# One decoder layer with routed experts, on one core: output projection and routing in one block, weight buffers shared, picks in batches of six tiles, block table through TensorE

## The reference

```python
mix = concatenate([y_conv, y_rec]) @ w_out
x = layer_norm(ALPHA * x + gate1 * mix, ln_g[0], ln_b[0])      # x1
u = x * (1.0 + scale2) + shift2                                # u2
# routing: top group of 4, top 2 of its 8 experts, 32 experts
p_group = softmax(xt @ w_rg); grp = argmax(p_group)
le = the 8 logits (xt @ w_re) of that group
top_p, top_i = top_k(softmax(le), 2)
wts = p_sel * top_p / sum(top_p)
# each expert: blocks of up to 128 tokens
h = silu(xblk @ w_gate[ex]) * (xblk @ w_up[ex]); y = h @ w_down[ex]
x = layer_norm(ALPHA * x + gate2 * y_moe, ln_g[1], ln_b[1])
```

## Time and profile before

| | us |
|---|---|
| median of 3 runs (1959.23 to 1959.64) | 1959.36 |
| the profiled execution, its own time | 1958.05 |
| its span | 1956.5 |

### The profile page before, as it was taken

How to read it: one execution, slowest core, us unless ns; L and a number is a source line. 1 busy time by engine, 2 the same in 40 slices (tenths; PEclk the granted TensorE clock), 3 DMA queues, 4 the chain that set the end, 5 groups by cost and what they waited for, 6 DMA issues and landing times. The chain is left out here.

```text
span 1956.5 us, 29481 instructions
## 1 busy us (share of the span) xinstructions
PE 1760.3 (90%) x9152; PEld 1374.9 (70%) x9153; DVE 1143.1 (58%) x1864; ACT 616.6 (32%) x770; POOL 597.1 (31%) x685
## 2 busy tenths in 40 slices
PE   5999999999999999999689989139999999999674
PEld 3888878888888899999478777127666777666331
DVE  4566665556666766565467778714456333455198
ACT  3333332222333222222211110205465434455142
POOL 0122222111222222102145556413444333344155
PEclk8999999999999999999799989569999999999897
DMA  8444334443333232331664342558899864798495
GB/s 262 140 141 131 115 99 139 131 133 111 98 99 91 87 87 59 90 108 41 218 187 151 130 130 98 166 176 275 282 358 339 310 231 167 252 315 301 194 387 182
DMA packets 302076, 342.76 MB, mean 175 GB/s; under 512 B 19077, under 2 KB 257446, under 8 KB 299537
## 3 DMA queue, kind: packets, MB, share of 16 engines
q1 hardware_dynamic: 278872, 284.30, 45.3%
q0 software_dynamic: 18000, 55.87, 7.9%
q10 hardware_dynamic: 5106, 1.31, 0.4%
HBM read 276.86 MB, written 64.58 MB: 175 GB/s over the span
## 5 line engine op out<-in xcount | busy, mean ns | idle before, releaser
L1534 DVE TENSOR_TENSOR w_gu_lo<-w_gu_raw,w_gu_hi (+1 forms) x64 | 146.4, 2291 | 158.3 <-ACT w_gu_hi L1527 158.2
L896 DVE TENSOR_TENSOR w_lo<-w_raw,w_hi 128x1024 fp32r<-128x1024 f32 x112 | 138.1, 1236 | 139.4 <-ACT w_hi L546 136.7
L658 POOL TENSOR_TENSOR o_r<-o_ms,neg_half 128x4 f32<-128x4 f32 (+1 forms) x16 | 16.8, 1051 | 663.0 <-DVEq L932 663.0
L1907 PE MATMUL ph<-w_gu_hi,x_hi 128*128 (+1 forms) x408 | 178.6, 438 | 12.9 <-DVE hh L1869 10.4
L713 PE MATMUL pr<-ub_hi,w_hi 128*128 128x288 f32 (+1 forms) x672 | 189.2, 335 | 0.0
L713 PE MATMUL pr<-ub_hi,w_lo 128*128 128x288 f32 (+1 forms) x672 | 184.2, 328 | 0.0
L713 PE MATMUL pr<-ub_lo,w_hi 128*128 128x288 f32 (+1 forms) x672 | 183.6, 327 | 0.0
L713 PE MATMUL pr<-ua_hi,w_hi 128*128 128x512 f32 x448 | 182.6, 408 | 0.0
L1935 PE MATMUL py<-w_dn_w,hhT 128*128 x400 | 180.9, 595 | 0.8 <-ACT hhT L1839 0.4
L713 PE MATMUL pr<-ua_hi,w_lo 128*128 128x512 f32 x448 | 177.0, 395 | 0.0
L713 PE MATMUL pr<-ua_lo,w_hi 128*128 128x512 f32 x448 | 176.9, 395 | 0.0
(11 more groups left out here) (334 smaller groups left out, 3482.5 us busy)
## 6 DMA issues: line engine op xcount, KB each, us to landing
w_raw<-in_w_in SPq DMA_DIRECT2D x112, 512.0 KB, 4.2
w_gu_raw<-in_w_e_gate SPq DMA_DIRECT2D x32, 1024.0 KB, 8.3
w_gu_raw<-in_w_e_up SPq DMA_DIRECT2D x32, 1024.0 KB, 11.9
w_dn_w<-in_w_e_down SPq DMA_DIRECT2D x32, 1024.0 KB, 10.1
w_mod<-in_w_mod SPq DMA_DIRECT2D x16, 1024.0 KB
y_t<-y_scratch SPq DMA_DIRECT2D x16, 1024.0 KB, 7.1
w_ring<-in_w_mod SPq DMA_DIRECT2D x4, 2048.0 KB, 17.4
x_cols<-in_x_prompt SPq DMA_DIRECT2D x32, 256.0 KB, 5.5
```

The source lines that it names most:

```text
L658: pool.tensor_tensor(o_r[:, 0:c], o_ms[:, 0:c], keep["neg_half"][:, 0:c], ALU.pow).then_inc(o_rs, 1)
L896: dve.tensor_tensor(w_lo[:, n % WS], w_raw[:, n % WRAW], w_hi[:, n % WS].bitcast(F32), ALU.subtract).then_inc(lo_done, 1)
L1534: dve.tensor_tensor(w_slot(keep["gu_lo"], s, lo, hi), w_slot(keep["gu_raw"], r, lo, hi), w_slot(keep["gu_hi"], s, lo, hi).bitcast(F32), AL ...
L1907: last = pe.matmul(ph[:, :], x[:, half, k * P:(k + 1) * P], w_slot(w, s, k * GU, (k + 1) * GU), start=(k == 0 and m == 0), stop=(k == KT - ...
```

## The change

- Output and routing become one block. The batches are (0,6), (6,12), (12,15) and (15,17); the first two are picked within the tile loop, the other two after it.
- In the tile loop, DVE's order per tile was residual, norm, `lo(t+3)`, picks; now it is residual, `lo(t+3)`, picks, norm. ACT makes `hi(t+2)` ahead of `to_sb(t-2)`, not behind it.
- u2 of tile 16 is made by DVE (`modulate_last`), not POOL.
- w_out, z, x1 and the transposes of u2 lie in the buffers of the gate and up weights (`gu_raw`, `gu_hi`, `gu_lo`). Gate and up weights of expert 0 are loaded at t = 8, those of 1 and 2 after the last logits; all three down weights are loaded in the expert phase.
- The table is transposed by two PE matmuls and copied by DVE from PSUM; it no longer goes to DRAM.
- Gate, norm weights and x1 of the first 8 tiles of the combine phase are loaded in the expert phase.

```diff
-    BATCH = ((0, 4), (4, 8), (8, 12), (12, 15))
+    BATCH = ((0, 6), (6, 12), (12, 15), (15, TILES))
...
-        wo_raw = sb("wo_raw", [P, KT, D])
+        wo_raw, wo_hi, wo_lo = (keep[n][:, 0:2, :].rearrange("p s (k d) -> p (s k) d", d=D) for n in ("gu_raw", "gu_hi", "gu_lo"))
+        mod_s = wo_raw[0:NSAMP, 4:7, :]
+        late = keep["gu_raw"][:, 2, :].rearrange("p (k d) -> p k d", d=D)
+        z, z2, x1 = late[:, 0, :], late[:, 1, :], late[:, 2:4, :]
...
                     if t + 2 < T:
                         load_x(t + 2)
+                    if t == 8:
+                        sp.wait_ge(list_out, 16)
+                        load_gate_up(sp, io, keep, 0, 0)
                     store(t)
...
+                sp.wait_ge(lg_ps, T)
+                for e in range(1, RAW):
+                    for landed in ("wg_in", "wu_in"):
+                        sp.wait_ge(keep[landed], 16 * e)
+                    load_gate_up(sp, io, keep, e, e)
...
                 for t in range(2, T):
-                    to_sb(t - 2)
                     if t + 2 < T:
                         hi(t + 2)
+                    to_sb(t - 2)
                     keep_logits(t - 2)
...
-                                scatter_rows(pool, R, scr, a + 2 * h, a + 2 * h + 2, sc_out)
+                                scatter_rows(pool, R, scr, a + 3 * h, a + 3 * h + 3, sc_out)
...
+                pe.wait_ge(tab_rdy, 1)
+                for c in range(2):
+                    last = pe.matmul(rk[0:1, c * P:(c + 1) * P], tab_f[:, c:c + 1], ident[:, :], start=True, stop=True)
+                last.then_inc(tab_ps, 1)
...
                 for t in range(T):
                     residual(t)
-                    norm(t)
                     if t + 3 < T:
                         lo(t + 3)
-                    dve.drain()
...
+                    norm(t)
+                    dve.drain()
...
+                modulate_last()
+                a, b = BATCH[2]
+                dve.wait_ge(lg_sb, b)
+                pick_groups(dve, R, a, b, gd_rdy)
+                pick_first(dve, R, a, b)
+                pick_second(dve, R, a, b, dm_rdy, mm_rdy)
+                place_rows(dve, R, rk, a, b, gs_rdy, w_rdy, rk_rdy, 2, dest_rdy)
...
-                sp.wait_ge(tab_rdy, 1)
-                sp.dma_start(scr["tab"], tab_i[:, :]).then_inc(tab_out, 16)
-                sp.wait_ge(tab_out, 16)
-                sp.dma_start(blk_tab[:, :], scr["tab"].rearrange("(a g) c -> a (g c)", a=1)).then_inc(tab_in, 16)
...
+                dve.wait_ge(tab_ps, 1)
+                dve.tensor_copy(blk_tab[:, :], rk[0:1, 0:2 * P])
                 dve.drain()
                 for e in range(2):
                     for a in range(2):
                         split_low(dve, keep, e, a, e, e)
...
+                for e in range(RAW):
+                    if e:
+                        sp.wait_ge(wd_in, 16 * e)
+                    load_down(sp, io, keep, e, e)
                 sp.wait_ge(xg_in, 32)
...
+                for t in range(EARLY):
+                    tail(NE - 2 + t // 4, t % 4, P, scr["x1"][t * P:(t + 1) * P, :])
```

More of the change, by code:

```diff
@@ L1310, in _ @@
                             pair_shares(act, R, a, b, w_rdy)
-                for t in range(T - 2, T):
-                    to_sb(t)
-                    keep_logits(t)
+                to_sb(LAST - 1)
+                keep_logits(LAST - 1)
+                act.wait_ge(gd_rdy, 3)
+                group_shares(act, R, *BATCH[2], gs_rdy)
+                to_sb(LAST)
+                keep_logits(LAST)
+                act.wait_ge(dm_rdy, 3)
+                pair_shares(act, R, *BATCH[2], w_rdy)
+                act.wait_ge(gd_rdy, 4)
+                group_shares(act, R, *BATCH[3], gs_rdy)
+                act.wait_ge(dm_rdy, 4)
+                pair_shares(act, R, *BATCH[3], w_rdy)
+                for e in range(2):
+                    act.wait_ge(keep["wg_in"], 16 * e + 16)
+                    act.wait_ge(keep["wu_in"], 16 * e + 16)
+                    for a in range(2):
+                        split_high(act, keep, e, a, e, e)
             @block.gpsimd
@@ L1365, in _ @@
                         pool.wait_ge(list_out, 16)
-                    for i, (a, b) in enumerate(BATCH[0:3]):
+                    for i, (a, b) in enumerate(BATCH[0:2]):
                         for h in range(2):
@@ L1424, in _ @@
                     route(t - 2)
-                    for i, (a, b) in enumerate(BATCH):
+                    for i, (a, b) in enumerate(BATCH[0:2]):
                         if t == b + 3:
@@ L1513, in load_gate_up @@
[L1513 to L1527, removed]
@@ L1758, in down, with tail @@
                     load_down(sp, io, keep, e, s)
+                def tail(e, i, n, rows):
+                    sp.wait_ge(gu_l, 2 * e + 2)
+                    sp.dma_start(gu_raw[0:n, e % RAW, i * D:(i + 1) * D], rows).then_inc(tail_in, 16)
+                for e in range(RAW):
+                    if e:
+                        sp.wait_ge(wd_in, 16 * e)
+                    load_down(sp, io, keep, e, e)
                 sp.wait_ge(xg_in, 32)
@@ L1765, in _ @@
                 down(NE - 1, (NE - 1) % RAW)
+                for i, row in enumerate((scr["mod"][0, 3 * D:4 * D], None, io["ln_g"][0, 1], io["ln_b"][0, 1])):
+                    if row is not None:
+                        tail(NE - 3, i, P, row_bcast(row, P))
+                for b in range(DEC_B):
+                    sp.dma_start(gu_raw[b * DEC_L:(b + 1) * DEC_L, (NE - 3) % RAW, D:2 * D],
+                                 row_bcast(scr["mod"][b + 1, 3 * D:4 * D], DEC_L)).then_inc(tail_in, 16)
+                for t in range(EARLY):
+                    tail(NE - 2 + t // 4, t % 4, P, scr["x1"][t * P:(t + 1) * P, :])
+                sp.wait_ge(tail_in, 16 * (3 + DEC_B + EARLY))
             @block.gpsimd
@@ L1886, in expert_of @@
                 def expert_of(b):
-                    return pe.value_load(blk_tab[0:1, bass.ds(2 * b, 1)], min_val=0, max_val=NE - 1)
+                    return pe.value_load(blk_tab[0:1, bass.ds(b, 1)], min_val=0, max_val=NE - 1)
                 def transposes(b, half):
@@ L1967, in combine_phase @@
         ps_n = ps("ps_n4", [P, D])
-        in_ = [sem("t4_in%d" % s) for s in range(R)]
+        y_in = [sem("y4_in%d" % s) for s in range(R)]
+        x_in = [sem("x4_in%d" % s) for s in range(R)]
         o_out = [sem("o_out%d" % s) for s in range(4)]
@@ L1975, in rows_of, with x1_of @@
             return NSAMP if t == LAST else P
+        def x1_of(t):
+            n = rows_of(t)
+            if t < EARLY:
+                return tail[0:n, t // 4, (t % 4) * D:(t % 4 + 1) * D]
+            return x1[0:n, (t - EARLY) % R, :]
         with nc.Block() as block:
```

221 lines of the change are left out of this document (92 added, 129 removed).

## The result

The changed kernel takes **1984.3 us** (median of 4 runs, 1980.4 to 1985.8), the one before 1959.5 (1959.2 to 1959.7). The ratio is 1.0124, with a 95% interval of 1.0106 to 1.0141: the change makes the kernel 24.8 us slower. The profiled execution has a span of 1982.7 us against 1956.5, 26.2 more.

The account below looks back on a forecast made before the run. PE was taken to bound the output phase before, and the ring after the change. Terms 43.4 - 14.8 + 4 - 1.3 = +31.3 on 1958.05 gave 1989.4, with 1.3 to the median 1991 us; range 1966 to 2012.

Parts of the forecast that it names:

- X(16): End of x1 of tile 16, the last in the output phase: forecast at 1273.5 us against 1230.1 before, +43.4.
- The ring: Tile loop: x1, u2, its store, next y load, hi, lo, norm, x1 set the pace, 16.2 us per tile; chance 0.68.
- X(0): End of x1 of tile 0, at the output phase's start: forecast at 995.5 us against 991.2 before.
- The picks: DVE's routing picks, now between lo and norm in the tile loop: 18.6 us added at t = 7, 8, 9 and 13.
- Scatters: Six on POOL behind u2 at t = 11 and 12 delay the root by 1.4 us each, 2.8 in all.
- The hole: Stretch between output phase and experts, X(16) to the first list fetch: 45.3 us instead of 60.1, -14.8.
- The first blocks: Start of the expert phase: down weight loads beside the list fetch and gather that PE awaits, +4 us, ends 0 and 10.
- Combine: Combine phase: fewer bytes to load ahead of PE at tile 0, -1.3 us, and no gain behind it, where DVE bounds.
- the clock: Rival: PE idles in every tile of the output phase and its clock falls; 17.3 us per tile, 2005 us, chance 0.20.
- The faster ring: The same as rival 3: in the tile loop the ring turns faster than PE; 1929 us, chance 0.08.
- the cancelling: Rival: the tile loop's loss is small and cancels the hole's gain, within 4 us of before; chance 0.04.
- rival 3: Output phase: u2 and load under 8.5 us together, PE stays the bound, picks hidden; 29 us less, 1929; chance 0.08.

Follow-up runs that it names:

- e9: The changed kernel with the picks of the tile loop behind norm(t), lo(t+3) still ahead of norm: 1969.7 us, ratio 1.0047.
- e5: e1 with DVE's four splits of the first two experts' weights moved behind the barrier, into the expert phase: 1928.4 us, ratio 0.9858.
- e1: The changed kernel with SP asking for each y piece one tile earlier, ahead of the stores: 1935.2 us, ratio 0.9877.
- e3: The kernel before with only DVE's lo(t+3) moved ahead of norm(t): 1989.7 us, ratio 1.0156.
- e7: The changed kernel without the eight x1 tiles loaded ahead of the combine phase: 1985.0 us, ratio 1.0137.
- e2: The changed kernel with only DVE's lo(t+3) moved back behind norm(t): 1936.7 us, ratio 0.9888.
- e10: The changed kernel with SP issuing the load of x(t+2) ahead of that of y(t+3): 2008.1 us, ratio 1.0239.

## Why the prediction was right

The forecast was 1991 us, the measured time 1984.3; the sum was +31.3 us on the profiled execution, and it shows +26.2. Term by term, from the two timelines:

| term | forecast | measured |
|---|---|---|
| X(16) | +43.4 | +45.0 |
| X(16) to the first list fetch | -14.8 | -15.4 |
| first fetch to first transposes | +4 | +0.8 |
| first transposes to combine | 0 | -1.8 |
| combine to first zw | -1.3 | -2.2 |
| first zw to the end | 0 | -0.2 |

- **The ring.** Forecast 16.2 us per tile; the turn shown takes 16.1. The terms as listed add up to 16.3 and not to 16.2, which is 1.2 us over twelve tiles and changes nothing else. The parts measured: u2 store 5.85 us behind X (forecast 6.1), SP 0.4, the y load 5.0 to the start of `hi` (median of the 13 loads of the loop, 4.1 to 8.0; the view of landings has only five of them, 4.1 to 6.6, median 4.8), and the same `hi`, `lo` and norm. The queueing that I assumed beside u2 is in the rows: POOL's first step runs to 1052.56, DVE's step with two SBUF operands, which asks at 1051.49, ends at 1053.64, so that its 1.23 us fit in only from 1052.4 on, within 0.15 us of POOL's end; POOL's addition, issued at 1052.71, ends at 1055.90, 2.3 behind that. By the Trainium skill, "SBUF — State Buffer", section "SBUF: two separate sides", the two engines hold their shared port pair in turns, each for a whole instruction; these rows agree, with 2.15 and 3.19 us where 1.23 and 2.34 stand alone.
- **The y load.** The Trainium skill's fit ("DMA: Bandwidth & Descriptors", section "Anatomy of one DMA — SWDGE (gpsimd) path"), which the prediction weighed, would by an estimate have made the load 3.2 us and the total some 20 us lower. Both traces have about 5 us, on SP's queue and beside other transfers: the row was the right one to go by.
- **Slow y loads.** One was forecast, beside the filling of the list: 8.6 instead of 4.8 us. It is there in the turn to tile 2, 8.0 us from issue to `hi`, and that turn took 19.1 us, 3.0 above 16.1 (forecast 3.8). Three more weren't: in the turns to tiles 5, 10 and 12 it took 6.2, 6.6 and 6.2 us, and the turns were 17.2, 17.6 and 17.3. What slowed these isn't shown.
- **X(0)** came 4.8 us behind the forecast of 995.5. Of these 3.2 were there before the phase began: SP issued its first y load at 954.68 against 951.46, behind phases whose instructions the diff leaves alone; why they took longer isn't shown. From X(0) to X(13) it took 231.3 us, forecast 234.0. So the two parts of X(16) are off by +4.8 and -2.7, and the agreement at X(16) is better than its parts.
- **The picks.** The turns with picks at t = 7, 8 and 9 took 21.0, 19.2 and 21.3 us: 4.9, 3.1 and 5.2 above 16.1 (forecast 5.1, 3.1, 5.3); the one at t = 13, with the half piece of y, 19.2 (forecast 19.5). e9 shows what their place costs.
- **Scatters** at t = 11 and 12: the turns took 16.4 and 17.3, forecast 17.6 each, and the step forecast for them is mostly wrong. The root behind six scatters held x1 of tile 11 for 0.53 us; at tile 12 it ended at 1209.06, while DVE was still in `lo`, and held nothing. The 1.2 us of that turn lie in the y load. So 0.5 us came the way forecast, of 2.8.
- **Tiles 14 to 16** took 43.5 us, forecast 44.0, with x1 of the last tile held 8.0 us for the root behind six scatters.
- **The hole.** 44.7, forecast 45.3. The table's way through PE, which the trace of before didn't show and which was taken as 1.6, took 1.5 from the matmuls to the end of the copy. The splits became the last link, as forecast; e5 takes them out.
- **The first blocks** are the term that was mis-sized: +4 forecast, +0.8 measured. I charged to the first list fetch what such a fetch takes more in the expert phase's traffic, 3.8 us. The down loads start at 1317.70, 2.1 us ahead of the first fetch, but POOL had to wait for it only 3.54 us against 2.69 before. In e1 this stretch took 10.1 us, in e3, without the down loads there, 9.1.
- **Expert phase.** -1.8 us is no effect that I can claim: with the same matmuls this stretch took 539.4 to 545.2 us over the twelve kernels. What makes it vary stays open.
- **Combine.** -1.3 forecast; -2.2 between the two profiled executions, and -1.4 between the means of the nine kernels with the changed phase and the three with the old one. The size is near, the mechanism isn't shown: the forecast gave it to x1 being there early, and e7, without those loads, keeps all but 0.3 us. That the term came out is luck.

Of the rivals, the clock (0.20) fell as what sets the time, but the granted clock did go down as PE waited more. The windows from about X(0) to X(13), the changed kernel and then e1:

```profile
1000.00:1231.00 231.00, 197.20 (x928) 161.18 (x929) 131.34 (x176) 28.45 (x45) 90.26 (x52) 0.91 0.40 132
1000.00:1180.00 180.00, 178.01 (x924) 150.33 (x925) 126.36 (x176) 27.69 (x44) 95.26 (x52) 0.99 0.51 166
```

Nearly the same matmuls take PE 197 us at a clock of 0.91 and 178 at 0.99. (A value between 0.50 and 1 is a mean of stretches at 1.2 and 2.4 GHz.) These 19 us are PE's busy time, not the kernel's: PE still had 34 us without work in that window, and no link of the ring is on PE. The faster ring (0.08) and the cancelling (0.04) fell too. But the hidden side of rival 3 is real: it gave 1929 us for a kernel in which PE stays the bound (1930 with the 1.3 us between profile and median that the forecast adds), and e1, which makes it so, took 1935.

## What to carry to other kernels

An in-order queue that feeds a late stage and stores an early one is a link like any other. When an instruction is moved ahead in one engine's order, follow from it backwards through every queue until you come to an older tile of the instruction that it was moved ahead of: if you get there, you have closed a ring, and the sum of its durations over the tiles that it spans is the new tempo. Compare it with the tempo of the engine that bounds (here 16.2 against 13.8 us), and count in it whatever else stands between its links; once it turns slower, every 0.1 us in it is paid once per tile, and an idle PE hides nothing. A gain elsewhere in the same change (15 us in the hole) says nothing on its parts: here one moved call cost some 47 us (e2), and the rest of the change was worth some 22.

## What the runs showed of the hardware that was not expected

- With one more 512 KB load issued 0.47 us ahead of it on the same queue, it took 6.3 us in the median from the issue of the y load to `hi`, instead of 5.0 (e10, 13 loads each).
- Scatters issued by POOL hold it for 0.96 us each with 0.30 between, and the first of six for 1.0 to 1.8 us: six of them stood for 8.2 us ahead of a 0.58 us operation that x1 of the last tile needed (rows of L2263 above).
- The loads of the down weights start 2.1 us ahead of the first list fetch, and POOL's wait behind that fetch was only 0.85 us longer than before, while list fetches took up to 9.0 us in the phase's later traffic. Why so little isn't shown.
